# Group A attention scores: the second pass on 64-row tiles of PE, two key halves on two row tiles

## What is computed

```python
qa = _axial_rope(_rmsnorm(qa.reshape(b, s, N_Q_A, HEAD_DIM), q_norm_a[i]), tables)
ka = _axial_rope(_rmsnorm(ka.reshape(b, s, N_KV_A, HEAD_DIM), k_norm_a[i]), tables)
out_a = _gqa_blocked(qa, ka, va)
...
def block(qblk):
    sc = jnp.einsum('bqkgd,bskd->bkgqs', qblk, k, preferred_element_type=jnp.float32) * scale
    p = jax.nn.softmax(sc, axis=-1).astype(v.dtype)
    return jnp.einsum('bkgqs,bskd->bqkgd', p, v)
```

## Time and profile before

| | us |
|---|---|
| median of three runs | 2245.26 |
| lowest, highest | 2231.58, 2245.31 |
| the profiled execution's own time | 2231.26 |
| its span | 2229.5 |
| group A in it | 351 to 601 |
| group B in it | 601 to about 790 |

### The profile page before, as it was taken

One profiled execution on the slowest core, in us unless ns is written; L12 is line 12 of the kernel. 1 busy time (PEld: TensorE's weight loads), 2 busy tenths in 40 slices (PEclk: granted clock), 3 DMA queues, 4 the chain that ended last, 5 costly groups with the idle time before them and its releaser, 6 DMA issues.

```text
span 2229.5 us, 29550 instructions
## 1 busy us (share of the span) xinstructions
PE 2148.5 (96%) x10684; PEld 1725.9 (77%) x10684; DVE 1516.8 (68%) x1966; ACT 743.7 (33%) x1185; POOL 303.7 (14%) x188
## 2 busy tenths in 40 slices
PE   7999999999989899999999999999999999987997
PEld 5777787777767688888888888888888888865885
DVE  6686635777656575767777767777777777775546
ACT  6222114666656631331222212122221212244223
POOL 6110101000011134300010100001000000023111
PEclk9999999999989899999999999999999999998998
DMA  5223347101088330010100100001010010110103
GB/s 175 109 90 131 138 146 189 35 15 28 23 156 165 62 151 29 29 38 29 37 28 28 38 28 31 35 29 37 28 38 28 28 38 28 38 47 19 48 29 113
DMA packets 54299, 140.04 MB, mean 63 GB/s; under 512 B 23009, under 2 KB 23521, under 8 KB 54241
## 3 DMA queue, kind: packets, MB, share of 16 engines
q1 hardware_dynamic: 53376, 138.14, 21.1%
q10 hardware_dynamic: 864, 1.13, 0.1%
HBM read 107.79 MB, written 31.46 MB: 62 GB/s over the span
## 4 chain that ended last, share of the span: by engine, by line
PE 87%; DVE 6%; ACT 2%; DMA 2%; issue 1%; SPq 1%; POOL 1%; DVEq 0%; ACTq 0%; POOLq 0%
PE ps L307 24%; PE ps L308 24%; PE ps L309 24%; PE ps L1137 3%; PE ps L1108 3%; PE ps L1091 2%; PE ps L1092 2%; DMA TR<-in_rpb 1%; DVE NL L1920 1%; PE ps L1155 1%; PE ps L1074 1%; PE ps L1057 1%; PE ps L1122 1%; PE ps L1101 1%; SPq L951 1%
## 5 line engine op out<-in xcount | busy, mean ns | idle before, releaser
L307 PE MATMUL ps<-NH,WH 128*128 128x512 f32 x1896 | 756.6, 399 | 20.2 <-DVE WL L682 9.3
L308 PE MATMUL ps<-NL,WH 128*128 128x512 f32 x1896 | 742.8, 392 | 0.0
L309 PE MATMUL ps<-NH,WL 128*128 128x512 f32 x1896 | 742.3, 392 | 0.0
L307 PEld LDWEIGHTS ps<-NH,WH 128*128 128x128 f32 x1896 | 358.8, 189 | 107.7 <-DVE NL L676 16.4
L308 PEld LDWEIGHTS ps<-NL,WH 128*128 128x128 f32 x1896 | 358.9, 189 | 79.0 <-issue 6.0
L309 PEld LDWEIGHTS ps<-NH,WL 128*128 128x128 f32 x1896 | 358.7, 189 | 75.7
L1852 DVE TENSOR_TENSOR H<-H,ps 128x512 f32<-128x512 f32 x480 | 305.5, 683 | 102.8 <-PE ps L309 102.8
L284 POOL TENSOR_TENSOR raw<-raw,gains 128x1024 f32<-128x1024 f32 x76 | 151.2, 1995 | 1326.2 <-DMA raw<-in_w 1326.2
L299 ACT ACTIVATE WH<-raw 128x1024 fp32r<-128x1024 f32 x102 | 107.8, 1057 | 572.7 <-PE ps L309 543.9
L307 PE MATMUL ps<-MH,WH 128*128 128x512 f32 x504 | 197.3, 392 | 8.1 <-DVE H L1927 6.4
L309 PE MATMUL ps<-MH,WL 128*128 128x512 f32 x504 | 196.6, 390 | 0.0
(11 more groups left out here) (180 smaller groups left out, 2429.7 us busy)
## 6 DMA issues: line engine op xcount, KB each, us to landing
raw<-in_w SPq DMA_DIRECT2D x102, 512.0 KB, 3.2
xst<-in_xT SPq DMA_DIRECT2D x24, 256.0 KB, 3.6
Q<-qkh SPq DMA_DIRECT2D x16, 384.0 KB, 6.3
H<-in_xT SPq DMA_DIRECT2D x8, 768.0 KB, 8.9
out_yT<-H SPq DMA_DIRECT2D x24, 256.0 KB, 2.1
qkh<-oqh SPq DMA_DIRECT2D x5, 768.0 KB, 3.3
qkl<-oql SPq DMA_DIRECT2D x5, 768.0 KB, 4.9
qkh<-obh SPq DMA_DIRECT2D x5, 768.0 KB, 3.3
```

The source lines that it names most:

```text
L307: nc.tensor.matmul(out, wh, xh, start=first, stop=False)
L308: nc.tensor.matmul(out, wh, xl, start=False, stop=False)
L309: return nc.tensor.matmul(out, wl, xh, start=False, stop=last)
```

## The change

In group A the second pass leaves out the product of the two low parts. It multiplies only the queries' high part with the keys' low part, over 64 rows. The first chunk of 512 keys reads partitions 0 to 63 (`QS`, `KL`), the second one partitions 64 to 127 (`Q2`, `KL`), so that the two matmuls of a long item stand on two row tiles of PE and write two banks. A short item has one chunk, on the first tile. Both first-pass matmuls of an item now come ahead of both second-pass ones. For this the queries' high part is loaded a third time in group A too, into partitions 64 to 127 of `Q2`, and `queries_landed` counts three loads. As these partitions also hold group B's mask, `load_masks(0)` moves from the start of stage 2 to the last pair of group A, after its half 0 is scored.

```diff
--- before.py
+++ after.py
@@ -846,7 +846,7 @@
 
         def queries_landed(kind, p):
 
-            return p * 32 + 32 if kind == "A" else (p - NPAIR_A) * 48 + 64
+            return p * 48 + 48 if kind == "A" else (p - NPAIR_A) * 48 + 64
 
         def values_landed(kind, p):
 
@@ -864,8 +864,7 @@
         def load_queries(kind, i, s):
             row = QROW[kind](i)[0]
             load_pieces((piece("qkh", row, s), piece("qkl", row, s)), QS[kind][s], q_ld[kind][s])
-            if kind == "B":
-                nc.sync.dma_start(Q2[s][0:DH, :], piece("qkh", row, s)).then_inc(q_ld["B"][s], 16)
+            nc.sync.dma_start(Q2[s][cols(kind == "A", DH), :], piece("qkh", row, s)).then_inc(q_ld[kind][s], 16)
 
         def load_keys(kind, i, s):
             row = QROW[kind](i)[1]
@@ -966,13 +965,13 @@
                 load_values("B", 0, s)
             load_queries("B", 0, 0)
             load_keys("B", 0, 0)
-            sp.wait_ge(mk_st, 16)
-            load_masks(0)
             load_table(0, 0)
             with sp.Fori(1, NPAIR_A) as i:
                 for s in range(2):
                     scored(i - 1, s)
                     load_queries("A", i, s)
+            scored(NPAIR_A - 1, 0)
+            load_masks(0)
             scored(NPAIR_A - 1, 1)
             load_keys("B", 0, 1)
             sp.wait_ge(pv_done, NPAIR_A * 6)
@@ -1084,12 +1083,15 @@
                 if m % 12 == 0:
                     pe.wait_ge(q_ld[kind][s], queries_landed(kind, p))
                     pe.wait_ge(k_ld[kind][s], keys_landed(kind, p))
-                q = QS[kind][s][:, g * GT + t * P:g * GT + (t + 1) * P].bitcast(F32R)
-                for c0 in range(0, w, GT):
-                    n = min(GT, w - c0)
-                    out = ps[:, 2 * (m % 2) + c0 // GT, 0:n]
-                    nc.tensor.matmul(out, q, KH[kind][s][:, k0 + c0:k0 + c0 + n].bitcast(F32R), start=True, stop=False)
-                    mm = nc.tensor.matmul(out, q, KL[kind][s][:, k0 + c0:k0 + c0 + n].bitcast(F32R), start=False, stop=True)
+                mine = slice(g * GT + t * P, g * GT + (t + 1) * P)
+                chunks = range(w // GT)
+                for c in chunks:
+                    nc.tensor.matmul(ps[:, 2 * (m % 2) + c, :], QS["A"][s][:, mine].bitcast(F32R),
+                                     KH["A"][s][:, k0 + c * GT:k0 + (c + 1) * GT].bitcast(F32R), start=True, stop=False)
+                for c in chunks:
+                    q = (QS["A"][s], Q2[s])[c]
+                    mm = nc.tensor.matmul(ps[:, 2 * (m % 2) + c, :], q[cols(c, DH), mine].bitcast(F32R),
+                                          KL["A"][s][cols(c, DH), k0 + c * GT:k0 + (c + 1) * GT].bitcast(F32R), start=False, stop=True)
                 mm.then_inc(s_rdy, 1)
 
             def turn(kind, p, m):
```

## The result

The changed kernel takes 2252.24 us (median of 20 runs, 2239.18 to 2261.82), the kernel before 2241.28 us (20 runs beside them, 2229.07 to 2248.43). The ratio is 1.0046, with a 95% interval of 1.0028 to 1.0064: 11 us slower, inside 1%, and clear of no change.

The account below looks back on a forecast made before the run. The prediction took PE to bound the kernel, busy 2148.5 of 2229.5 us. Its terms, -14.9 + 25.6 + 12.8 - 8.0 = +15.5 us on a median of 2245.3, gave 2260.8 us, range 2232 to 2284.

Parts of the forecast that it names:

- within 1%: Whole run: the time stays within about 22.5 us of the kernel before; chance 0.65.
- Side by side: Long items' second pass: two 64-row matmuls share one 0.23 us slot, saving 14.9 us.
- Changes of shape: Around the KL pass: two per item at 0.20 us each, +25.6 us for long items, +12.8 for short.
- the signs: Long item's timeline: 0.33 us to the first KL load, KL matmuls within 0.02, transposes' load 0.33 behind.
- Waits covered: PE's waits for PA copies and osum in group A absorb 1.0 us per half, -8.0 us.
- Order, loads, masks: KH chunks before KL, one more DMA per pair and half, later mask loads for B: no added time.
- The absolute number: Whole run: 2260.8 us, from the median of the timed runs, 2245.3, plus 15.5.
- Rival A: Group A scores: shape changes hidden and tiles side by side, faster, 2232 us; chance 0.12.
- Rival B: KL pass: row tiles don't overlap or load in series, slower, 2268 or 2274 us; chance 0.21.
- Rival C: Short items' stretches: clock falls to half rate, some 10 us more, 2271 us; chance 0.08.
- Rival D: Group A: more waits covered and the gain whole, time within 5 us of before; chance 0.07.

Follow-up runs that it names:

- e2: The changed kernel with both KL matmuls of a long item on the first row tile; ratio 1.0094 to the kernel before, half 34.2 us.
- e1: The changed kernel with the second pass over all 128 rows instead of row tiles; ratio 1.0002 to the kernel before, half 31.2 us.
- e5: The changed kernel with KH and KL passes alternating per chunk, four shape changes per long item; one run, 2283.21 us beside 2240.01.
- e3: The changed kernel with row tiles for long items alone, short items' second pass over all rows; ratio 1.0010 to the kernel before.
- e7: The kernel before with the probabilities' transposes on two row tiles, scores untouched; ratio 0.9977 to the kernel before, half 31.1 us.
- e4: The changed kernel with a row tile for short items alone, long items' second pass over all rows; ratio 1.0039 to the kernel before.
- e9: The kernel before with DVE copying group A's transposes ahead of the minimum of item m + 2; ratio 1.0111 to the kernel before.
- e6: The changed kernel with the probabilities' transposes on two row tiles too; ratio 1.0012 to the kernel before, half 31.3 us.
- e10: e3 with KL first for four long items per half and the rinv row moved ahead of the weighing; ratio 1.0109 to the kernel before.
- e8: e6 with DVE copying group A's transposes ahead of the minimum of item m + 2; ratio 1.0036 to the kernel before.
- e11: e10 with KL first for only two long items per half and the rinv row left behind the weighing; ratio 0.9995 to the kernel before.

## Why the prediction was right, and where it was off

The direction, the mechanism and the range held: 2252.2 lies between 2232 and 2284, "within 1%" was the likeliest case, and the ratio is clear on the slower side. Forecast +15.5 us, measured +11.0 (2252.24 - 2241.28); group A of the two profiles differs by 11.5.

1. *Side by side: right.* The pair starts together, and e2 prices it: 0.23 us per long item on PE, as in the sum, of which 0.20 arrive in the time.
2. *Changes of shape: right in kind, 12% too dear.* The step said 0.20 us each, from 0.09 of emptying and 0.11 of an exposed load. The short items, which have nothing else, give 0.35 for two: 0.175. Ahead of KL the full 0.20 is there (0.09 in the step from KH to KL, 0.11 in the step from KL to the transposes, which is 0.43 and not the 0.33 of the signs: the KL record begins together with its own exposed load). Ahead of the transposes the exposed load is 0.06, not 0.11; why it is less is not shown. So +11.2 instead of +12.8 us for the short items, and a net of +0.13 instead of +0.167 for a long one, +8.3 instead of +10.7 us. PE's extra is 19.5 us, not 23.5; this mis-sized term is 4.0 of the 4.5 us between forecast and result.
3. *Waits covered: right in sum, not in its parts.* Of 2.44 us more per half on PE (8 x 0.13 + 4 x 0.35) the steady half shows 1.38, so 1.06 fell into waits, 1.0 predicted; in the halves that follow the first one 1.1 to 1.4 did. The waits view agrees: 1.1 us now, from 2.2. But I had expected the copies' waits gone and osum's halved; of the copies' 1.2 us 0.2 is left, and osum kept 0.9 of its 1.0.
4. *Order, loads, masks: nothing.* e1 confirms it, 1.0002.
5. *The absolute number* was 8.6 us too high. 4.0 of it was the base: the median of three runs, 2245.3, is 2241.3 over 20.

Rival A (changes hidden) is out by the 23 gaps of a half and by e5. Rival B (tiles in series) is out by e2. Rival C, the clock, took some part, and not where it was put: the steady half, short items included, ran at 1.00. But the windows of 351 to 361 and 361 to 371 us of the changed kernel have a mean clock of 0.61 and 0.88, which is 10.2 us at the half rate, where the earlier trace rows have 6.8; the first half of pair 0 grew by 2.4 us and not by 1.3. So 1 to 2 of the 11.5 us are a clock that the sum had at nothing. Whether the change causes it stays open: by the same windows it is 6.8 us in e1, e3 and e7, 10.2 in e4, 16.6 in e2 and none in e9. Rival C's price doesn't follow from its own numbers either: half of eight stretches of 10 us is 40 us of work, and the half rate would add 40 us, not 10; the upper edge of the range, 2284, rests on that. Rival D is out by the interval: it had more waits covered and the time within 5 us of before, and the interval starts at 0.28%, 6 us.

## What to carry to other kernels

Two 64-row matmuls on two row tiles do run in one slot, but going there and back costs about 0.35 us, more than the one 512-column slot (0.23) that a pair saves. By these numbers tiling pays on PE when several pairs share one trip (the first item of e6, 1.56 us against 1.79), and breaks even when the work ahead of it has another shape anyway (e10's item, 1.01 us against 1.00); no kernel here turned that into a clearly shorter time. Price a change of shape from the trace before, at any place where the shape already changes, and count the changes per item, also in the items that gain nothing. And where one engine's stream has small waits for others, part of any addition to it vanishes in them, and so does part of any saving: e6, e8 and e11 freed PE time that came back as waits.

## What the runs showed of the hardware that I had not expected

The spread of whole runs, 14 us in the first three, goes with the granted clock. In the 20 runs of the changed kernel the time goes with the mean clock (correlation -0.89): 2239.18 us at 0.983 and 2261.29 at 0.973. The two profiled executions differ by 30.5 us of span, 2229.5 and 2260.0, at clocks of 0.981 and 0.973, and only 11.5 us of it lie in group A; the other 19.0 are outside, where the programs are the same. The clock accounts for most of them: the share withheld, 1.9% of 2229.5 us and 2.7% of 2260.0, is 18.7 us apart, 1.7 of them at the start of group A. From 780 to 1000 us, for one, the windows have 0.98 before and 0.93 in the changed kernel. Of e1, which is no slower than before, the profiled execution was one of 2250.04 us at 0.974. A single pair of profiles would have told nearly three times the loss of the medians; what decides the half rate in one execution and not in the next stays open.

Two weight loads on two row tiles also start together (443.70 twice), and so do 64-row transposes: 16 of them span 0.66 us in e6, 8 full ones 1.04 in the earlier trace rows.
